# One stage for the recurrence's projections and gates, and expert tiles split by row group

## The reference, cut to what matters

```python
def rwkv_mix(p, S0, mu, w0, w_up, a0, a_up, g_up, k_k, k_a, r_k, gn_g, gn_b):
    xs = (p + (centred_shift(p) - p) * mu).astype(F32)
    r, k, v, xw, xa, xg = split_cols(xs, (RWKV_DIM, RWKV_DIM, RWKV_DIM, DECAY_LORA, AAA_LORA, GATE_LORA))
    g = jax.nn.sigmoid(xg) @ g_up
    kk = (k * k_k).reshape(B, T, H, N)
    kk = kk * lax.rsqrt(jnp.sum(kk * kk, axis=-1, keepdims=True) + 1e-12)
    for d in range(2):
        w = -jax.nn.softplus(-(w0[d] + jnp.tanh(xw) @ w_up[d])) - 0.5
        decay = jnp.exp(-jnp.exp(w)).reshape(B, T, H, N)
        a = jax.nn.sigmoid(a0[d] + xa @ a_up[d]).reshape(B, T, H, N)
        kd = k.reshape(B, T, H, N) * (1.0 + (a - 1.0) * k_a.reshape(H, N))
        s_fin, yd = wkv_scan(rh, decay, kd, vh, -kk, kk * a, S0[d], reverse=(d == 1))
...
    for gi in range(N_GROUPS):
        hg = jnp.einsum('td,edf->tef', h, w_gate[e])
        hu = jnp.einsum('td,edf->tef', h, w_up[e])
        y = y + jnp.einsum('tef,efd->td', jax.nn.silu(hg) * hu * combine[:, e, None], w_down[e])
```

## Time and profile before

| | us |
|---|---|
| median of 3 runs (lowest, highest) | 2529.75 (2522.52, 2530.09) |
| profiled execution | 2523.77 |
| its span, first to last instruction | 2522.1 |
| PE busy | 2213.0 (88%) |
| DVE / ACT / POOL busy | 743.7 / 489.6 / 289.2 |
| mean granted TensorE clock | 0.954 of full |

### The profile page before, as it was taken

One profiled execution on the slowest core, in us unless ns is written; L12 is line 12 of the kernel. 1 busy time (PEld: TensorE's weight loads), 2 busy tenths in 40 slices (PEclk: granted clock), 3 DMA queues, 4 the chain that ended last, 5 costly groups with the idle time before them and its releaser, 6 DMA issues. The chain is left out here.

```text
span 2522.1 us, 58728 instructions
## 1 busy us (share of the span) xinstructions
PE 2213.0 (88%) x26490; PEld 1411.1 (56%) x26490; DVE 743.7 (29%) x1634; ACT 489.6 (19%) x1088; POOL 289.2 (11%) x467
## 2 busy tenths in 40 slices
PE   6989998899979999999999788996999799987774
PEld 2444443799824444445555464544889688744443
DVE  1023323767541111220000022436676311300001
ACT  2022302433210000300111132304332101210001
POOL 0000000333200000010111100001343000011111
PEclk8989999899989999999999989998999999998987
DMA  7129807000022121447999821200000244799994
GB/s 267 67 101 332 321 17 237 3 4 4 4 84 83 68 98 69 167 146 278 383 385 383 306 81 40 81 29 1 4 4 4 85 150 169 273 333 381 379 384 141
DMA packets 182934, 400.23 MB, mean 159 GB/s; under 512 B 6656, under 2 KB 29952, under 8 KB 182496
## 3 DMA queue, kind: packets, MB, share of 16 engines
q1 hardware_dynamic: 170528, 361.94, 39.9%
q0 software_dynamic: 8576, 23.08, 2.5%
q10 hardware_dynamic: 3648, 12.45, 1.7%
HBM read 365.47 MB, written 31.98 MB: 158 GB/s over the span
## 5 line engine op out<-in xcount | busy, mean ns | idle before, releaser
L471 PE MATMUL ps<-H,memory 128*128 128x512 f32 (+2 forms) x1728 | 611.5, 512 | 9.7 <-issue 9.7
L471 PEld LDWEIGHTS ps<-H,memory 128*128 128x128 f32 (+1 forms) x1728 | 328.8, 191 | 281.1 <-issue 263.4
L697 PE MATMUL ps<-memory 64*64 64x64 f32 (+1 forms) x12672 | 386.4, 223 | 40.1 <-issue 16.0
L697 PEld LDWEIGHTS ps<-memory 64*64 64x64 f32 x12672 | 366.7, 136 | 56.2 <-issue 33.9
L471 PE MATMUL ps<-memory 128*128 128x512 f32 (+4 forms) x960 | 340.6, 505 | 18.2 <-DVE memory L1387 10.6
L940 PE MATMUL ps<-memory 128*32 128x256 f32 x5120 | 307.4, 403 | 49.1 <-DMA memory<-in_eu 47.5
L940 PEld LDWEIGHTS ps<-memory 128*32 128x32 f32 x5120 | 183.5, 116 | 169.2 <-issue 77.1
L471 PEld LDWEIGHTS ps<-memory 128*128 128x128 f32 (+2 forms) x960 | 176.4, 186 | 172.1 <-issue 142.8
L961 PE MATMUL ps<-memory 128*32 128x256 f32 x2560 | 144.8, 380 | 17.8 <-ACT memory L1269 17.8
L1812 POOL TENSOR_TENSOR memory<-memory,cons 128x256 f32<-128x256 f32 x160 | 128.4, 815 | 193.0 <-DVE memory L1512 138.6
L961 PEld LDWEIGHTS ps<-memory 128*32 128x32 f32 x2560 | 81.1, 110 | 73.7 <-ACT memory L1269 12.9
(11 more groups left out here) (250 smaller groups left out, 1789.3 us busy)
## 6 DMA issues: line engine op xcount, KB each, us to landing
memory<-in_eg SPq DMA_DIRECT2D x32, 2048.0 KB, 16.3
memory<-in_eu SPq DMA_DIRECT2D x32, 2048.0 KB, 21.3
memory<-in_ed SPq DMA_DIRECT2D x32, 2048.0 KB, 20.8
memory<-in_w_ada SPq DMA_DIRECT2D x24, 2048.0 KB, 10.3
memory<-in_w_in SPq DMA_DIRECT2D x20, 2048.0 KB, 9.1
expert_rows<-memory SPq DMA_DIRECT2D x4, 3456.0 KB, 24.0
memory<-in_w_out SPq DMA_DIRECT2D x4, 2048.0 KB, 8.4
memory<-expert_rows ACTq DMA_DIRECT2D x19, 384.0 KB, 6.9
```

Source lines behind the costliest of these rows:

```text
L471: ins = mm(ps[0:M, bank, 0:w], lhs(k), rhs(k), start=(k == 0), stop=(k == n - 1))
L697: ins = mm(out[cols, j], lhs[rows, j, :], rhs[rows, j], start=(n == 0), stop=(n == len(terms) - 1))
```

## The change

It does two things.

The two stages ahead of the recurrence become one. The tiles come in the order of `RIN_ORDER`: keys, decay/rate, gate, r, v. The keys' sums follow the next tile's products, and gate unit `u` follows projection `8 + u`; units 6 and 7 come last. The weights are loaded in that order. `DA` is now one tile of 512 columns with the decay input on partitions 0 to 63 and the rate input on 64 to 127, and each of the two products of a unit takes 64 partitions of it, so nothing has to be zero. The mixing's scratch moves to `MIXED`. A handover between the stages is gone.

In the expert loop the next tile's token rows are transposed in two halves, one ahead of the hidden values' transposes and one behind. ACT copies the hidden values ahead of the token rows. With three groups (layer 0) SiLU, multiplication and hidden transposes are done for the first two groups and for the third apart.

```diff
+RIN_ORDER = [4, 5, 6, 7, 12, 13, 0, 1, 2, 3, 8, 9, 10, 11]
-L_THIRD = ("R", "K", "V", "WAG", "LORA") + ...
+L_THIRD = ("K", "WAG", "R", "V", "LORA") + ...
-        DA = place(SCR, 2)
+        DA, MIXED = memory[:, 2048:2560], memory[:, 3072:3584]
...
+                load(l, "R", rows(w_in[l, :, C_R:C_R + 512], KD), KD, 512, *third[2])
+                load(l, "V", rows(w_in[l, :, C_R + 1024:C_R + 1536], KD), KD, 512, "rin_ready", RT * l + 4)
+                load(l, "LORA", lora[l].rearrange("p (k n) -> p k n", k=1), 1, 1536, "rin_ready", RT * l + 6)
... PE
+                def key_sum(j):
+                    pe.wait_ge(sem("key_squares"), RJ * l + j + 1)
+                    mm(ps[:, 4 + j, :], hsum, B[0][:, j, :], start=True, stop=True).then_inc(sem("key_sums"), 1)
+
+                def lora_up(u):
+                    if u == 0:
+                        loaded(pe, l, "LORA")
+                        pe.wait_ge(sem("decay_input"), l + 1)
+                    if u < 2:
+                        pe.wait_ge(sem("key_rstd"), RJ * l + 2 * u + 2)
+                    else:
+                        pe.wait_ge(sem("lora_gates"), 16 * l + 2 * u - 2)
+                    j, d = u // 2, u % 2
+                    for half in range(2):
+                        hh = slice(64 * half, 64 * half + 64)
+                        mm(ps[:, 4 + 2 * (u % 2) + half, :], slot(l, "LORA")[hh, d * RD + j * P:d * RD + j * P + P], DA[hh, :],
+                           start=True, stop=True).then_inc(sem("lora_up"), 1)
+
+                for i, o in enumerate(RIN_ORDER):
...
+                    if i >= 4:
+                        pe.wait_ge(sem("rin_copied"), RT * l + i - 3)
+                    product(i % 4, rin_width(l, o), ...).then_inc(sem("rin_ready"), 1)
+                    if 1 <= i <= RJ:
+                        key_sum(i - 1)
+                    if i >= RT - 6:
+                        lora_up(i - RT + 6)
+                for u in range(6, 2 * RJ):
+                    lora_up(u)
                 handover("pe", pe)
... PE, expert loop
                         ins.then_inc(sem(f"tile_up{b}"), 1)
                         wait_apart(pe, f"rows_loaded{1 - b}", 16 * (it + 1 + b + (2 * l if b else l)))
-                        turn_rows(1 - b)
-                        pe.wait_ge(sem("tile_hidden"), jt + 1)
+                        turn_rows(1 - b, 0)
                         for g in range(groups):
+                            if g in (0, groups - 1):
+                                pe.wait_ge(sem("tile_hidden"), 2 * jt + (1 if g == 0 and groups == 3 else 2))
                             ins = pe.transpose(ps[:, 4, g * P:g * P + P], HID[:, 0, g * P:g * P + P], ident)
                         ins.then_inc(sem("hidden_turned"), 1)
+                        turn_rows(1 - b, 1)
                         pe.wait_ge(sem("hidden_copied"), jt + 1)
... ACT
+                for i, o in enumerate(RIN_ORDER):
+                    act.wait_ge(sem("rin_ready"), RT * l + i + 1)
+                    if i >= 2:
+                        act.wait_ge(sem("rin_mixed"), RT * l + i - 1)
...
+                    if 1 <= i <= RJ:
+                        act.wait_ge(sem("key_sums"), RJ * l + i)
+                        rsqrt(B[1][:, i - 1, :], ps[:, 3 + i, :], 1, 1).then_inc(sem("key_rstd"), 1)
...
+                    if i >= RT - 6:
+                        gates(i - RT + 6)
+                for u in range(6, 2 * RJ):
+                    gates(u)
                 act.preload_act_table_set("natural_log_exp_and_others")
... ACT, expert loop
+                        if groups == 3:
+                            act.wait_ge(sem("tile_part"), jt + 1)
+                            act.activation(three(SIL)[:, 0:2], gates[:, 0:2], ACT.Silu).then_inc(sem("tile_silu"), 1)
+                            act.wait_ge(sem(f"tile_up{b}"), it + 2)
+                            act.activation(three(SIL)[:, 2:3], gates[:, 2:3], ACT.Silu).then_inc(sem("tile_silu"), 1)
... DVE
+                for i, o in enumerate(RIN_ORDER):
...
+                    if i < RJ:
+                        key_squared(i)
+                    if 2 <= i <= RJ + 1:
+                        dve.wait_ge(sem("key_rstd"), RJ * l + i - 1)
+                        link(tt(KK[:, i - 2, :], KK[:, i - 2, :], B[1][:, i - 2, :], ALU.mult))
+                    if i >= RT - 6:
+                        gates(i - RT + 6)
+                for u in range(6, 2 * RJ):
+                    gates(u)
                 over()
... DVE, expert loop
+                            tt(three(HID)[:, 0:2], three(SIL)[:, 0:2], ups[:, 0:2], ALU.mult).then_inc(sem("tile_hidden"), 1)
+                            dve.wait_ge(sem("tile_silu"), 2 * jt + 2)
+                            tt(three(HID)[:, 2:3], three(SIL)[:, 2:3], ups[:, 2:3], ALU.mult).then_inc(sem("tile_hidden"), 1)
```

More of the change, by code:

```diff
@@ L80 @@
 L_SECOND = ("F", "Q", "KV", "DFT", "UKV")
-L_THIRD = ("R", "K", "V", "WAG", "LORA") + tuple(f"MERGE{n}" for n in range(12)) + ("OUT0", "OUT1", "SG", "SU", "SD")
+L_THIRD = ("K", "WAG", "R", "V", "LORA") + tuple(f"MERGE{n}" for n in range(12)) + ("OUT0", "OUT1", "SG", "SU", "SD")
 LOADS = [("ADA", n) for n in range(EARLY)] + [(x, 0) for x in L_SECOND] + \
@@ L394, in _ @@
                     third = [("ada_rows", 2 * N_ADA - 2 + n) for n in range(NSLOT)]
-                load(l, "R", rows(w_in[l, :, C_R:C_R + 512], KD), KD, 512, *third[0])
+                load(l, "K", rows(w_in[l, :, C_R + 512:C_R + 1024], KD), KD, 512, *third[0])
                 if l:
@@ L398, in _ @@
                         head_weights(l, h)
[L399 to L402, removed]
+                load(l, "WAG", rows(w_in[l, :, C_R + 1536:C_R + 1792], KD), KD, 256, *third[1])
+                load(l, "R", rows(w_in[l, :, C_R:C_R + 512], KD), KD, 512, *third[2])
+                load(l, "V", rows(w_in[l, :, C_R + 1024:C_R + 1536], KD), KD, 512, "rin_ready", RT * l + 4)
+                load(l, "LORA", lora[l].rearrange("p (k n) -> p k n", k=1), 1, 1536, "rin_ready", RT * l + 6)
                 def gate(b, g):
@@ L656, in _ @@
                 handover("pe", pe)
-                for o in range(RT):
+                def key_sum(j):
[15 more added lines that the diff above has]
+                for i, o in enumerate(RIN_ORDER):
                     n, j = ("R", "K", "V", "WAG")[o // 4], o % 4
@@ L662, in _ @@
                         loaded(pe, l, n)
-                    if o >= 8:
-                        pe.wait_ge(sem("rin_copied"), RT * l + o - 7)
-                    product(o % 8, rin_width(l, o), weights(l, n, 256 if n == "WAG" else 512, j), lambda k: H[:, k, 0:rin_width(l, o)], KD)\
+                    if i >= 4:
+                        pe.wait_ge(sem("rin_copied"), RT * l + i - 3)
+                    product(i % 4, rin_width(l, o), weights(l, n, 256 if n == "WAG" else 512, j), lambda k: H[:, k, 0:rin_width(l, o)], KD)\
                         .then_inc(sem("rin_ready"), 1)
[L667 to L681, removed]
+                    if 1 <= i <= RJ:
[4 more added lines that the diff above has]
+                    lora_up(u)
                 handover("pe", pe)
@@ L913, in _, with turn_rows @@
                 groups = tr // GROUP
-                def turn_rows(b):
-                    for k in range(KD):
+                def turn_rows(b, half):
+                    for k in range(4 * half, 4 * half + 4):
                         ins = pe.transpose(ps[:, k // 4, (k % 4) * P:(k % 4) * P + tr], XG[0:tr, b, k * P:k * P + P],
                                            ident[0:tr, 0:tr])
-                    return ins.then_inc(sem(f"rows_turned{b}"), 1)
+                    if half:
+                        ins.then_inc(sem(f"rows_turned{b}"), 1)
                 pe.wait_ge(sem("route_ready"), l + 1)
@@ L925, in _ @@
                 wait_apart(pe, "rows_loaded0", 16 * (pairs_before + 2 * l + 1))
-                turn_rows(0)
+                for half in range(2):
+                    turn_rows(0, half)
                 with pe.Fori(0, pairs) as i:
@@ L1094, in _, with gates @@
                 handover("act", act, act.copy(dummy[:, 1:2], epst[:, 0:1]))
[L1096 to L1113 removed]
+                def gates(u):
                     j, d = u // 2, u % 2
@@ L1795, in _ @@
                 ins.then_inc(sem("rin_padded"), 1)
+                pool.memset(Y[:, :, :], 0.0)
                 over()
-                pool.memset(Y[:, :, :], 0.0)
                 for d in range(2):
                     pool.memset(ONCE["S"][d], 0.0).then_inc(sem("state"), 1)
-                over()
                 def blocks(k, n, d):
```

75 lines of the change are left out of this document (36 added, 39 removed).

## The result

| | before | after |
|---|---|---|
| median of the runs | 2527.76 (2522.52 to 2530.09, 4 runs) | 2491.21 (2488.71 to 2493.63, 4 runs) |
| profiled execution, and its span | 2523.77, 2522.1 | 2488.71, 2487.0 |
| mean granted clock | 0.954 | 0.953 |

The ratio is 0.9863, 95% interval 0.9847 to 0.9879: the kernel is 36.6 us faster by the medians, 35.1 by the two profiled executions. The forecast was 2488, with 2477 to 2501 as its range.

What follows compares the result with a forecast made beforehand. PE, busy 88% of the span, was taken to bound the kernel, so its waits cost time. Savings of 35.4 us (both stages) and 3.2 (layer 0's loop), 38.6 from 2526.5, gave 2488 us, range 2477 to 2501.

Steps and rivals of the forecast that it cites:

- The tail behind the last projection: Last projection to scan: DVE's mixing, 2.9 us, and three gate units at 1.85 remain, 8.7 us (8.4 to 10.5).
- What PE gets between the projections: Projections, per layer: key sums 3.4, five gate pairs 4.3 and shape changes 1.2 add 8.9 us (8 to 14).
- The change of shape: Gate units among projections: switching the products' shape costs PE 0.12 us each time, 1.2 for ten.
- The stage's saving: Stretch ahead of the scan: 18.2 us saved in layer 0 and 17.2 in layer 1, together 35.4.
- The moved loads and the clears: Later loads of v and LORA, and POOL's clearing of Y and the state, cost nothing.
- The expert loop of layer 0: Tiles 0.7 us shorter, 11.2 in all, but up-weight transfers stop the gain from tile 8, leaving 3.2 us.
- Layer 1's loop: Layer 1's expert loop: two unsplit groups, PE waits for weights, transposes' order off the chain; gain 0 (up to 0.3).
- A: Gate units: a unit's halves don't overlap, 4.3 us more per layer, saving 30.0, about 2496 us; chance 0.13.
- B: Layer 0's expert loop: weights land earlier, so it gains all 11.2 us, saving 46.6, about 2480 us; chance 0.09.
- C: Projections: PE waits for the gate chain on ACT and DVE; kernel slower, about 2537 us at 12 per iteration; chance 0.03.
- D: Scan: removed wait returns there; longer low clock costs 2 us per layer, 2492 us; counted within the forecast's range.
- The sum: Whole kernel: 35.4 us from the two stages plus 3.2 from layer 0's loop, 38.6 saved, 2488 us.

Runs made afterwards that it cites:

- two units per projection: Changed kernel with two gate units behind each of projections 8 to 11, none behind the last: 2485.99 us, ratio 0.9818; timed again 2484.81 us, 0.9831.
- the whole products: Changed kernel, but each gate unit's two products take all 128 partitions against a DA with zero halves: 2497.32 us in one run.
- the kernel without the split: Changed kernel with SiLU and multiplication on all three groups at once in layer 0, token-row transposes still in halves: 2497.42 us in one run.
- the loop alone: Kernel before with only the change's expert-loop part, its two stages left apart: 2527.19 us, ratio 0.9999.
- the lighter loads: Only half of each up weight matrix loaded for tiles 2 to 15 in layer 0: 2525.33 us on the kernel before, 2476.55 us on the changed kernel.
- the stage alone: Changed kernel with the expert loop of before, so only the merged stage: 2493.32 us, ratio 0.9839.

## Why the prediction held, step by step

**The tail behind the last projection** (forecast 8.7, measured 8.67 in both layers). It was built from DVE's instructions alone, 2.9 and three times 1.85, and DVE's rows after show that chain. Right in size and mechanism, and two units per projection confirm it by taking three units out.

**What PE gets between the projections** (forecast 8.9, measured 9.7). Key sums at 0.86: exact. Pairs at 0.86, full overlap: right, by the two pairs in 1.92 and by the whole products, which cost 0.65 more. The scan's row that it was taken from shows 1.15 for a serial 1.7, that is, some overlap and not a full one; to take the lower of the two bounds was a choice that came out well. The change of shape was the mis-sized term. It was taken at 0.12 from attention's rows; here it is 0.20 going in and 0.19 coming back, so ten cost 1.95 in place of 1.2. That is 0.75 per layer, nearly all that this part missed by. Of projections a small slip: the row from which 0.856 was worked out begins at the window's edge; the whole row starts at 323.95 and gives 0.860 a product. It changes no term by more than 0.1.

The Trainium skill's page TensorE: Matmul & The Clock Gate, section Single matmul latency, with its fixed 166 ns, led to an estimate of 1.7 for these ten changes. The page gives that figure for a single product, as what its issue, drain and the rest take at full clock, and not for a change of shape. The measured 1.95 lies nearer to it than to the row that was preferred, and each change costs a little more than the page's figure. The page TensorEngine Tiling (Array Packing), section Key Properties, says that a change of tiling mode drains TensorE; that each change costs 0.20 or 0.19, and two pairs in a row only one of each, agrees with it.

**The stage's saving** (forecast 18.2 and 17.2, measured 17.4 and 16.5 in the trace). Together 33.9 in place of 35.4.

**The moved loads and the clears** (forecast nothing): nothing. PE doesn't wait in the stage's first 106 us. The tables of functions leave the path too; ACT loads the next one at 434.86, beside DVE's units.

**The expert loop of layer 0** (forecast 3.2, measured 2.1). The tile's gain was forecast at 0.7 and is 18.06 - 17.37 = 0.69, but this exactness is in part luck. The forecast put nothing on the halves of the token rows (they fit into the copy's time) and all of the 0.7 on the rest; the kernel without the split shows a loss of 0.13 for the halves and 0.83 for the split, and the two misses cancel. The cap by memory was forecast to bite at tile 8; tile 7 begins 0.3 late and tile 8 waits 1.67. What was mis-sized is what the cap leaves. SP's issues of the up weights of tiles 2 and 15 in the changed kernel (against the earlier trace rows), and their landing (against the earlier trace rows):

```profile
1138.89 0.53 SPq L439 DMA_DIRECT2D memory<-in_eu  x1
...
1371.61 9.21 SPq L439 DMA_DIRECT2D memory<-in_eu  x1
```

```profile
memory<-in_eu SPq DMA_DIRECT2D x1, 2048.0 KB, 16.9
...
memory<-in_eu SPq DMA_DIRECT2D x1, 2048.0 KB, 25.5
```

They landed at 1155.8 and 1397.1: 18.56 us per tile, against 18.48 before. The transfers didn't move up with the earlier need; over 13 tiles they even took 1.1 longer. The slack of 2.7 at tile 15 had been that of before, and it came out smaller by just this. Why the transfers are a trace slower is not settled.

In the other executions of the changed kernel the loop took 289.26 and 290.00, so the gain is 0.9 to 2.1, and by the runs of the loop alone it can't be told from nothing.

**Layer 1's loop** (forecast 0, measured 0.4 shorter): PE's waits for the up weights there are 49.9 in 13 waits, against 47.5 in the earlier trace rows. PE's wait for the multiplication rose, and the one for the copy is gone. PE's waits in that loop, in the changed kernel and then in the kernel before:

```profile
PE ps L952 <- DMA memory<-in_eu: 49.9, 13, 6.9
...
PE ps L964 <- DVE memory L1779: 11.1, 16, 0.7
```

```profile
PE ps L961 <- ACT memory L1269: 8.7, 16, 0.6
PE ps L949 <- DVE memory L1741: 5.0, 16, 0.3
```

The statement that the order of transposes is off the chain was wrong: it costs 0.06 per tile from up to down products (9.08 from one start to the other, 9.02 before). The wait for weights hides it, and the total forecast of nothing holds for that reason alone: the loop takes 273.3 in place of 273.7. Its first tile had a granted clock of 1.00 after and 0.83 before; from the second on it is 260.7 against 259.7, and the executions with the loop of before reach from 259.7 to 261.7 there.

**The rivals.** A, halves that don't overlap: false, 0.86 a pair. Had it been so, a layer would have been 4.3 longer; the whole products, which need no change of shape, make it 2.3 longer. B, memory gives way: false, and the lighter loads show what it would have brought, 11.2 in the loop. C, the gate chain paces PE: false in every run. D, the removed wait comes back as a longer low clock at the scan: false. Over the first 15 us of the scan the granted clock was 0.59 and 0.66 before (layer 0, layer 1), 0.58 and 0.65 in the changed kernel, 0.58 and 0.66 with two units per projection. The first long row of products in layer 0's scan, before and then in the changed kernel:

```profile
463.16 6.25 PE L697 MATMUL ps<-memory 64*64 64x64 f32 x128 [5.11 <-DVE memory L1506]
```

```profile
444.97 6.41 PE L707 MATMUL ps<-memory 64*64 64x64 f32 x128 [5.11 <-DVE memory L1538]
```

These 128 records take 6.25 before, 6.41 in the changed kernel and 6.37 with two units per projection, where the idle time ahead of the scan is 3.62, 5.13 and 3.16. So a shorter gap doesn't lift the clock here. In layer 1 the low clock begins a little earlier: the scan's first 32 records took 1.15 before and take 1.97 now.

```profile
1713.30 1.97 PE L707 MATMUL ps<-cons,memory 64*64 64x64 f32 x32 [5.12 <-issue]
```

**The sum** (38.6 forecast from 2526.5; 36.6 measured by medians). Rightly predicted in mechanism, with two terms too large: 1.5 in the stage and 1.1 in the loop. The account of the two traces leaves 0.9 us of other stretches, which hold larger movements of both signs. The largest, 2.4, is in layer 1's attention. The same 15 instructions of PE, kernel before:

```profile
1562.38:1567.45 5.07, 5.07 (x15) 2.12 (x15) 3.16 (x9) 1.56 (x4) 0.00 (x0) 1.00 0.00 0
```

and the changed kernel:

```profile
1541.53:1548.29 6.76, 6.76 (x15) 2.82 (x15) 3.10 (x9) 1.56 (x4) 0.00 (x0) 0.75 0.00 0
```

The clock's column falls from 1.00 to 0.75, a part of the stretch at the lower of the two levels, and the work takes 1.7 us more. A second such spell just ahead of layer 1's projections stretches 16 records, that is 8 products, from 1.96 to 3.37. Over all kernels that ran, the stretch from loop to projections took 198.5 to 198.8 us in three (the kernel before, two units once, the kernel before with lighter loads) or 200.0 to 201.0 in the nine others, without any edit in it. What decides between the two isn't settled. Both executions that have neither part of the change are among the three, and nine of the ten with one part or both are among the others, so that some 2 us may be a cost of the change; but two units per projection took 198.8 once and 200.9 once.

## What to carry to other kernels

A gap in which the busiest engine waits for a chain on the others is best removed by moving that chain between the engine's own long work: its length after is then the part of the chain that needs the last result, and it can be summed from instruction durations to a tenth. Then spread the chain so that as little as possible depends on the last result; doubling units earlier and leaving none behind gave 3.3 us more per layer here. Before shortening the compute of a loop, compare the landing period of its weights with its own period: a loop whose weights land every 18.5 us keeps little of a tile that could run in 17.4.

## What the runs showed of the hardware

Two fp32 products of 512 columns on 64 partitions each, in two different halves of TensorE's rows and into two PSUM banks, take 0.86 us together, the time of one on 128 partitions. Going into and out of that shape costs 0.20 and 0.19 us, whether one pair or two stand between.

The same kernel's untouched parts move from one execution to the next. Three profiled executions of the changed kernel had spans of 2487.0, 2489.8 and 2496.9, while its two merged stages agreed within 0.1. In layer 0's expert loop the first tile's up products took 12.25 us in three executions of the changed kernel and in the kernel before, and 10.57 in the kernel with the stage alone, with the same instructions ahead; the granted clock over them was 0.86 in the kernel before and in the first execution of the changed kernel, 1.00 with the stage alone. How much of all the movement is the clock's was not worked out. A difference of a few microseconds between two traces is read from the stretch that was edited, not from the span.
